# Gate maps of a PEER layer: one-hots of the first key on three engines, VectorE's instructions over eight tokens

## The reference

```
e1 = jnp.take_along_axis(i1, si // PEER_TOPK, axis=-1)
e2 = jnp.take_along_axis(i2, si % PEER_TOPK, axis=-1)
experts = e1 * N_KEYS + e2
gates = jax.nn.softmax(sv, axis=-1)
a = jnp.einsum('cd,ced->ce', h_c, u[e_c])
act = jax.nn.gelu(a, approximate=False) * g_c
return jnp.einsum('ce,ced->cd', act, v[e_c])
```

## Time and profile before

| | |
|---|---|
| runs of the kernel | 2482.23 us median of 3 (2481.68 to 2483.88) |
| the profiled execution | 2480.07 us, span 2478.3 us, mean granted clock of TensorE 0.982 |
| busy: PE, DVE, ACT, POOL | 93%, 70%, 52%, 9% of the span |
| chain that ended last | PE 81%, POOL 9%, DVE 5%, ACT 3% |
| line 432, GpSimd | 256 instructions, 212.5 us busy |
| lines 1425, 1429, 1437, VectorE | one-hots of i1, one-hots of i2, applies |
| line 1036, ScalarE | 512 instructions, 162.5 us busy, 390 ns each |

### The profile page before, as it was taken

One profiled execution on the slowest core, in us unless ns is written; L12 is line 12 of the kernel. 1 busy time (PEld: TensorE's weight loads), 2 busy tenths in 40 slices (PEclk: granted clock), 3 DMA queues, 4 the chain that ended last, 5 costly groups with the idle time before them and its releaser, 6 DMA issues.

```text
span 2478.3 us, 47911 instructions
## 1 busy us (share of the span) xinstructions
PE 2302.9 (93%) x15320; PEld 2099.6 (85%) x15320; DVE 1723.4 (70%) x3637; ACT 1284.0 (52%) x2842; POOL 226.9 (9%) x285
## 2 busy tenths in 40 slices
PE   5998999999996699999899999999999976999998
PEld 5896899999996588888788878999999965788887
DVE  7575666888868966666635557458888879666665
ACT  3454345455556755555546553445555567555554
POOL 0000000000007900000000000000000059100000
PEclk8998999999998999999999999999999989999999
DMA  9650354555550065555323324445555510455554
GB/s 371 260 196 35 107 199 148 183 178 184 184 183 25 0 203 194 191 191 193 128 102 136 120 103 142 145 143 182 185 180 184 179 67 0 144 195 192 191 192 152
DMA packets 106078, 389.71 MB, mean 157 GB/s; under 512 B 12032, under 2 KB 12160, under 8 KB 105232
## 3 DMA queue, kind: packets, MB, share of 16 engines
q1 hardware_dynamic: 104688, 381.73, 44.8%
q10 hardware_dynamic: 992, 4.88, 0.5%
q0 software_dynamic: 320, 2.13, 0.2%
HBM read 387.64 MB, written 1.05 MB: 157 GB/s over the span
## 4 chain that ended last, share of the span: by engine, by line
PE 81%; POOL 9%; DVE 5%; ACT 3%; DMA 1%; issue 1%; SPq 0%; POOLq 0%; DVEq 0%; ACTq 0%
PE ps L580 19%; PE ps L542 16%; PE ps L547 16%; PE ps L544 16%; PE ps L584 9%; POOL scores L432 9%; DMA big<-ada_in 1%; DVE act_lo L1272 1%; DVE lo L1195 1%; DVE big L1279 1%; PE ps L694 1%; PE ps L641 1%; PE ps L661 1%; DVE act_hi L1271 1%; ACT hi L923 0%
## 5 line engine op out<-in xcount | busy, mean ns | idle before, releaser
L923 ACT ACTIVATE hi<-raw 128x512 fp32r<-128x512 f32 x1356 | 776.5, 620 | 79.3 <-PE ps L547 77.0
L1195 DVE TENSOR_TENSOR lo<-raw,hi 128x512 fp32r<-128x512 f32 x844 | 547.0, 689 | 186.7 <-ACT hi L923 185.8
L542 PE MATMUL ps<-act_hi,hi 128*128 128x256 f32 x3376 | 553.3, 287 | 22.4 <-ACT hi L923 15.2
L547 PE MATMUL ps<-act_hi,lo 128*128 128x256 f32 x3376 | 546.6, 285 | 11.1 <-DVE lo L1195 11.1
L544 PE MATMUL ps<-act_lo,hi 128*128 128x256 f32 x3376 | 545.8, 284 | 0.0
L542 PEld LDWEIGHTS ps<-act_hi,hi 128*128 128x128 f32 x3376 | 468.5, 193 | 37.4 <-issue 20.2
L547 PEld LDWEIGHTS ps<-act_hi,lo 128*128 128x128 f32 x3376 | 469.0, 193 | 12.6 <-DVE lo L1195 12.6
L544 PEld LDWEIGHTS ps<-act_lo,hi 128*128 128x128 f32 x3376 | 468.8, 193 | 0.0
L1471 DVE TENSOR_TENSOR lo<-raw,hi 128x512 fp32r<-128x512 f32 x512 | 329.9, 688 | 131.4 <-ACT hi L923 124.2
L950 ACT ACTIVATE big<-ps 128x256 f32 (+1 forms) x346 | 133.1, 385 | 537.8 <-PE ps L547 537.8
L580 PE MATMUL ps<-hi,act_hi 128*128 128x512 f32 x1024 | 399.0, 390 | 0.0
(11 more groups left out here) (183 smaller groups left out, 1407.1 us busy)
## 6 DMA issues: line engine op xcount, KB each, us to landing
raw<-u SPq DMA_DIRECT2D x256, 512.0 KB, 4.2
raw<-v SPq DMA_DIRECT2D x256, 512.0 KB, 3.4
raw<-front SPq DMA_DIRECT2D x166, 512.0 KB, 3.5
big<-ada_in SPq DMA_DIRECT2D x48, 512.0 KB, 5.5
big<-biasA_in ACTq DMA_DIRECT2D x1, 2048.0 KB, 9.3
xT<-xT_in ACTq DMA_DIRECT2D x1, 1024.0 KB, 10.4
big<-keys_in ACTq DMA_DIRECT2D x1, 1024.0 KB, 12.7
scores<-memT_in POOLq DMA_DIRECT2D x1, 1024.0 KB, 5.4
```

The lines of the kernel that those rows point to most:

```text
L542: pe.matmul(out_ap, hi_l(k), hi_r(k), start=(first and k == 0), stop=False, skip_group_check=True)
L547: mm = pe.matmul(out_ap, lo_l(k), hi_r(k), start=False, stop=(last and k == n - 1), skip_group_check=True)
L923: act.activation(hi[:, s, :, :], raw[:, rs, 4 * h:4 * h + 4, :], ACT.Copy).then_inc(hi_done, 1)
L1195: dve.tensor_tensor(lo[:, s, :, :], raw[:, rs, 4 * h:4 * h + 4, :], hi[:, s, :, :].bitcast(F32), ALU.subtract).then_inc(lo_done, 1)
```

## The change

It does four things.

- The one-hots of i1 are shared by three engines, per group of 16 tokens: VectorE makes map 0 (4 tokens), GpSimd map 1 and two tokens of map 3 (`POOL_HOTS`), ScalarE map 2 and the other two tokens of map 3 (`ACT_HOTS`).
- GpSimd's and ScalarE's one-hots of i1 are scaled by the gate when they are made. GpSimd compares and multiplies in one instruction with two scalar columns. ScalarE takes two instructions per token: the distance |key - iota| (Abs), and Relu(gate - gate x distance), which is the gate where the distance is zero and zero elsewhere, as the gate is positive; it reads `neg_gate`, a new tile that VectorE makes before `ch_t`. Only map 0 still has its one-hots of i2 scaled by ScalarE, four instructions per group instead of 16.
- VectorE makes the one-hots of i2 of two maps (eight tokens) in one instruction of 1024 columns, and applies two maps, which lie in two neighbouring banks, in one instruction. `w_done` and `hot2` count pairs.
- The tile `zeros` of 256 columns becomes four columns, which its readers repeat.

```diff
@@ -46,6 +46,8 @@
 LN_EXP = "natural_log_exp_and_others"
 EXP_TANH = "exp_and_others"
 MAPS = 4
+POOL_HOTS = ((1, 4), (3, 2))
+ACT_HOTS = ((2, range(4)), (3, range(2, 4)))
 
 
 class Run:
@@ -176,7 +178,8 @@
         ones = sb("ones", [P, P])
         blockones = sb("blockones", [P, P])
         iota = sb("iota", [P, P])
-        zeros = sb("zeros", [P, T])
+        zero = sb("zero", [P, 4])
+        neg_gate = sb("neg_gate", [P, T])
         cols = sb("cols", [P, N_COLS])
         mod = sb("mod", [P, 48])
         gain = sb("gain", [P, 2, KT])
...
@@ -424,17 +428,17 @@
                 pool.wait_ge(ch_t, b)
 
                 for g in range(64 // MAPS):
-                    for j in range(1, MAPS, 2):
+                    for j, n in POOL_HOTS:
                         if g:
                             pool.wait_ge(wmap, 64 * (b - 1) + MAPS * (g - 1) + j + 1)
-                        for t in range(4):
+                        for t in range(n):
                             tok = 4 * MAPS * g + 4 * j + t
-                            ins = pool.tensor_scalar(onehot[:, j, t, :], iota[:, :], chosenT[:, 0, tok:tok + 1], None,
-                                                     ALU.is_equal)
-                        ins.then_inc(hot_odd, 1)
+                            ins = pool.tensor_scalar(onehot[:, j, t, :], iota[:, :], chosenT[:, 0, tok:tok + 1],
+                                                     chosenT[:, 2, tok:tok + 1], ALU.is_equal, ALU.mult)
+                        ins.then_inc(hot_pool, 1)
 
             link(pool.memset(ones[:, :], 1.0))
-            link(pool.memset(zeros[:, :], 0.0))
+            link(pool.memset(zero[:, :], 0.0))
             link(pool.memset(eps[:, :], EPS))
             link(pool.memset(ident[:, :], 0.0))
             link(select(ident[:, :], [[-1, P]], 0, 1, 1.0, ALU.not_equal))
...
@@ -706,10 +710,18 @@
                 def body(g):
                     for j in range(MAPS):
                         n = g * MAPS + (64 * (b - 1) + j)
-                        pe.wait_ge(hot_odd if j % 2 else hot_even, g * (MAPS // 2) + (32 * (b - 1) + j // 2 + 1))
-                        pe.wait_ge(hot_gate, n + 1)
-                        if not is_static(n) or n >= MAPS:
-                            pe.wait_ge(w_done, n - MAPS + 1)
+                        if j == 0:
+                            pe.wait_ge(hot_first, g + (16 * (b - 1) + 1))
+                            pe.wait_ge(hot_scaled, g + (16 * (b - 1) + 1))
+                        for k, (slot, _) in enumerate(POOL_HOTS):
+                            if slot == j:
+                                pe.wait_ge(hot_pool, g * len(POOL_HOTS) + (64 // MAPS * len(POOL_HOTS) * (b - 1) + k + 1))
+                        for k, (slot, _) in enumerate(ACT_HOTS):
+                            if slot == j:
+                                pe.wait_ge(hot_act, g * len(ACT_HOTS) + (64 // MAPS * len(ACT_HOTS) * (b - 1) + k + 1))
+                        pe.wait_ge(hot2, g * 2 + (32 * (b - 1) + j // 2 + 1))
+                        if not is_static(g) or g > 0 or b > 1:
+                            pe.wait_ge(w_done, g * 2 + (32 * (b - 1) + j // 2 - 1))
                         for t in range(4):
                             mm = pe.matmul(maps[j][:, t * P:t * P + P], onehot[:, j, t, :], gatehot[:, j, t, :],
                                            start=True, stop=True)
@@ -727,7 +739,7 @@
 
                 pe.wait_ge(ch_t, b)
                 for d in range(KT):
-                    pe.matmul(acc[:, d, :], zeros[:, 0:P], zeros[:, :], start=(d % 2 == 0), stop=False,
+                    pe.matmul(acc[:, d, :], zero[:, 0:1].broadcast_to([P, P]), zero[:, 0:1].broadcast_to([P, T]), start=(d % 2 == 0), stop=False,
                               skip_group_check=True)
                 run(f"v{b}")
                 for half in range(2):
@@ -1029,19 +1041,34 @@
                 act.wait_ge(ch_t, b)
 
                 def gate_hots(g):
-                    for j in range(MAPS):
-                        act.wait_ge(hot2, g * MAPS + (64 * (b - 1) + j + 1))
-                        for t in range(4):
+
+                    act.wait_ge(hot2, g * 2 + (32 * (b - 1) + 1))
+                    for t in range(4):
+                        ins = act.activation(gatehot[:, 0, t, :], gatehot[:, 0, t, :], ACT.Copy,
+                                             scale=chosenT[:, 2, bass.ds(g * 4 * MAPS + t, 1)])
+                    ins.then_inc(hot_scaled, 1)
+                    n = sum(len(tokens) for _, tokens in ACT_HOTS)
+                    done = 64 // MAPS * n * (b - 1)
+                    for j, tokens in ACT_HOTS:
+                        if not is_static(g):
+                            act.wait_ge(wmap, g * MAPS + (64 * (b - 1) - MAPS + j + 1))
+                        for t in tokens:
+                            act.activation(onehot[:, j, t, :], iota[:, :], ACT.Abs, scale=-1.0,
+                                           bias=chosenT[:, 0, bass.ds(g * 4 * MAPS + (4 * j + t), 1)])\
+                                .then_inc(hot_abs, 1)
+                        for t in tokens:
+                            done += 1
                             tok = g * 4 * MAPS + (4 * j + t)
-                            ins = act.activation(gatehot[:, j, t, :], gatehot[:, j, t, :], ACT.Copy,
-                                                 scale=chosenT[:, 2, bass.ds(tok, 1)])
-                        ins.then_inc(hot_gate, 1)
+                            act.wait_ge(hot_abs, g * n + done)
+                            ins = act.activation(onehot[:, j, t, :], onehot[:, j, t, :], ACT.Relu,
+                                                 scale=neg_gate[:, bass.ds(tok, 1)], bias=chosenT[:, 2, bass.ds(tok, 1)])
+                        ins.then_inc(hot_act, 1)
 
                 gate_hots(0)
                 with act.Fori(1, 64 // MAPS) as g:
                     gate_hots(g)
                 r = RUNS[f"v{b}"]
-                act.wait_ge(w_done, 64 * b)
+                act.wait_ge(w_done, 32 * b)
 
                 def body(g):
                     for j in range(GROUP):
...
@@ -1411,40 +1438,40 @@
                     .then_inc(gate_done, 1)
                 dve.wait_ge(ch_tr, b)
                 for c in range(3):
-                    ins = dve.tensor_copy(chosenT[:, c, :], bx[c][:, 0:T])
-                link(ins)
+                    dve.tensor_copy(chosenT[:, c, :], bx[c][:, 0:T])
+                link(dve.tensor_scalar(neg_gate[:, :], bx[2][:, 0:T], -1.0, None, ALU.mult))
                 dve.engine_nop().then_inc(ch_t, 1)
 
                 dve.wait_ge(taken, r.out0 + r.outs)
 
-                def hots(g, j):
-
-
-                    if j % 2 == 0:
-                        key = chosenT[:, 0, bass.ds(g * 4 * MAPS + 4 * j, 4)]
-                        dve.tensor_tensor(onehot[:, j, :, :], iota[:, :].unsqueeze(1).broadcast_to([P, 4, P]),
+                def hots(g, pair):
+
+                    key = chosenT[:, 1, bass.ds(g * 4 * MAPS + 8 * pair, 8)]
+                    dve.tensor_tensor(gatehot[:, 2 * pair:2 * pair + 2, :, :].rearrange("p b t n -> p (b t) n"),
+                                      iota[:, :].unsqueeze(1).broadcast_to([P, 8, P]),
+                                      key.unsqueeze(2).broadcast_to([P, 8, P]), ALU.is_equal).then_inc(hot2, 1)
+                    if pair == 0:
+                        key = chosenT[:, 0, bass.ds(g * 4 * MAPS, 4)]
+                        dve.tensor_tensor(onehot[:, 0, :, :], iota[:, :].unsqueeze(1).broadcast_to([P, 4, P]),
                                           key.unsqueeze(2).broadcast_to([P, 4, P]), ALU.is_equal)\
-                            .then_inc(hot_even, 1)
-                    key = chosenT[:, 1, bass.ds(g * 4 * MAPS + 4 * j, 4)]
-                    dve.tensor_tensor(gatehot[:, j, :, :], iota[:, :].unsqueeze(1).broadcast_to([P, 4, P]),
-                                      key.unsqueeze(2).broadcast_to([P, 4, P]), ALU.is_equal).then_inc(hot2, 1)
-
-                def apply(g, j):
-
-                    n = g * MAPS + (64 * (b - 1) + j)
-                    dve.wait_ge(wmap, n + 1)
-                    d = dense[:, :, bass.ds(g * 4 * MAPS + 4 * j, 4)]
-                    dve.tensor_tensor(d, maps[j].rearrange("p (t i) -> p i t", t=4), d, ALU.mult)\
-                        .then_inc(w_done, 1)
-
-                for j in range(MAPS):
-                    hots(0, j)
+                            .then_inc(hot_first, 1)
+
+                def apply(g, pair):
+
+                    dve.wait_ge(wmap, g * MAPS + (64 * (b - 1) + 2 * pair + 2))
+                    d = dense[:, :, bass.ds(g * 4 * MAPS + 8 * pair, 8)]
+                    first = (6, 0)[pair]
+                    dve.tensor_tensor(d, ps[:, first:first + 2, :].rearrange("p b (t i) -> p i (b t)", t=4), d,
+                                      ALU.mult).then_inc(w_done, 1)
+
+                for pair in range(2):
+                    hots(0, pair)
```

(10 more changed lines are left out.)

9 lines of the change are left out of this document (5 added, 4 removed).

## The result

The changed kernel takes 2496.32 us, median of four runs (2494.98 to 2498.41); the kernel before took 2481.95 in four runs beside it (2480.71 to 2483.88). The ratio is 1.0059, with a 95% interval of 1.0043 to 1.0075. So the change costs 14.4 us where 7 us of gain were forecast. The time lies above the range, on the other side of no change, and on the 2496 that the GpSimd rival had with the upper end of its price. The profiled execution took 2494.98 us, span 2493.1, mean granted clock 0.976 (before 0.982).

What follows compares the result with a forecast made beforehand. GpSimd was taken as the bound, to be replaced by a circle of waits: per block 0.35 + 6.3 + 15 x 6.2 + 1.5 + 2.75 = 103.9 us against 107.6, two blocks -7.4, giving 2475 us, range 2468 to 2489.

Steps and rivals of the forecast that it cites:

- the GpSimd rival: GpSimd's six one-hots per group become the bound again, from a load of 6.45 us: 2487 or 2496 us, chance 0.18.
- GpSimd's load: GpSimd's six one-hots per group, with second column and waits behind VectorE: 5.8 us, ends 5.1 and 7.7.
- the circle: Loop of waits through VectorE, ScalarE and TensorE, apply to next apply of maps 0 and 1: 6.19, taken as 6.2 us.
- the sign of "wrong": Prediction wrong if a GpSimd instruction alone exceeds 0.79 us, VectorE's 1024 columns 1.3, or even-part clock is below 0.95.
- The sign of the GpSimd rival: In the new profile, GpSimd without gaps and above 1.05 us per instruction would show GpSimd as the bound.
- The second column: GpSimd's one-hots: extra for a second scalar column and multiply, taken as 0.1 us each, ends 0 and 0.29.
- The waits: GpSimd held up by VectorE instructions with two SBUF inputs, in proportion to columns: 1.7 us per group.
- The prediction's other price: GpSimd's hold-up if a 1024-column VectorE instruction always costs its full length: 1.07 us each, 2.5 per group.
- VectorE and ScalarE: Their loads per group: VectorE 5.1 us, ScalarE 5.3 us, with 0.30 per distance or scaling and 0.38 per Relu.
- The first apply: Start of each block's stretch: first apply begins 6.3 us in, set by TensorE at its lower clock level.
- The end of the stretch: From the last apply of maps 0 and 1, through maps 2 and 3, to the zero matmuls: 2.75 us.
- The clock: TensorE's granted clock: 1.00 in the even part, one fall after the first group, counted as 1.5 us per block.

Runs made afterwards that it cites:

- The PSUM version of the kernel before: Kernel before the change, with only `iota`, the row of key numbers VectorE compares with, copied to a PSUM bank: 2460.91 us, ratio 0.9919.
- the version with one column: Changed kernel, but GpSimd's six one-hots per group only compare, with one scalar column and no multiply: 2475.35 us, ratio 0.9975.
- the versions at 6.32: Changed kernel with GpSimd's one-hots only comparing (2475.35 us), with `iota` in PSUM (2475.51), or with one token moved from GpSimd to ScalarE (2479.86).
- the split over four tokens: Changed kernel with VectorE's instructions back over four tokens: 2490.40 us; with `iota` in PSUM as well: 2441.28 us.
- either part of the change alone: Changed kernel with VectorE's instructions back over four tokens: 2490.40 us; kernel before with only VectorE's i2 one-hots and applies paired: 2507.06 us.

## Why the prediction was wrong, point by point

**What bounds the kernel now: right.** GpSimd did, and VectorE stood close behind it. The PSUM version of the kernel before shows the distance: 6.56 to 5.98.

**GpSimd's load, "6 x (0.58 + 0.1) + 1.7 = 5.8 us": this is the step that failed.** It measured 6 x 0.785 + 2.1 = 6.8, so GpSimd stayed the bound and the circle did not take over. Two terms were undersized, and by the sum both are needed. With 0.19 for the second column and 1.7 of waits the load would be 6 x 0.77 + 1.7 = 6.3, just at the circle; with 0.1 and 2.1 it would be 6.2. The load passed 6.45, the point from which the GpSimd rival decided, and went on to the 6.9 for which that rival had 2496. The prediction had set the sign of "wrong" at more than 0.79 us for an instruction alone; it measured 0.78 to 0.79 (0.797 at most with `iota` in PSUM), just at that sign. The sign of the GpSimd rival came plainly: 1.14 us per instruction, above its 1.05, and hardly a gap.

*The second column.* Taken 0.1, measured 0.19 (780 against 593 ns, with nothing else changed). I had put it near zero because one short read is small beside a tensor read. The multiply over 128 elements was counted at nothing, and there was no reason for that. The upper end of 0.29, the difference of a whole instruction to a select, is itself a slip (597 - 288 is 0.31; 0.29 is 0.58 - 0.288). The 0.19 lies halfway between it and the 0.1 taken. With the middle of both ranges, 0.145 for the column and 2.05 for the waits, the load would have been 6.4, above the circle.

The Trainium skill, GPSIMD Engine Reference, section 7 (Performance pitfalls for Q7 kernels), gives about 102 cycles for a small read command, from which the prediction had worked out the estimate of 0.085 us. The runs show 0.19 for column and multiply together; how it divides was not measured. A rule on the price of a read is no price of an instruction with one read more and one operation more.

*The waits.* Taken 1.7 per group, measured 2.1. The prediction had said that an apply does not hold GpSimd up and one-hots with both inputs in SBUF do. That is shown: with `iota` in PSUM no instruction of GpSimd exceeds 0.82 us. The size came from columns, 0.32 us per 512. That does not hold: the same 2560 columns cost 2.1 us in two instructions of 1024 and one of 512 and also in five of 512, 2.3 in the former cut beside the shorter instruction of GpSimd, and 1.3 (5 x (1.048 - 0.785)) where GpSimd has five tokens. What a wait costs goes by where it starts: in the version with one column 30 instructions start 0.03 to 0.04 us before a 1024 that a 512 follows and each takes 1.64, that is 1.04 more than the 0.60 alone; with five tokens 30 start 0.36 us into one and take 2.04, 1.25 more than 0.785. The prediction's other price, 1.07 for a 1024, is close to the first, though no row of it gives that figure.

The Trainium skill, SBUF — State Buffer, "Who interferes with whom", calls the shared port an exclusive lock. The trace agrees: one instruction of GpSimd stands through two of VectorE (2.26 us) and one, at the start of each block, through three (3.34 us). By the lock in full I had 2.5 us and a load of 6.6; measured 2.1 and 6.8. The rule was nearer than my proportion, and it should have had more than its part of 0.18.

**The circle, 6.19 us: nearly right.** It is 6.32. Apply to one-hots 1.15, one-hots 1.21, two maps 2.05, scalings 1.28, TensorE to VectorE 0.14 were as computed. ScalarE started 0.16 us after the one-hots ended instead of 0.13, and TensorE 0.33 after the scalings (807.57 against 805.96 + 1.28) instead of 0.24: the handover had been read behind GpSimd and was used behind ScalarE. At 6.32 in each round and the load in time, the time is the forecast's: 2475.35 and 2475.51 were measured.

**VectorE and ScalarE: right.** 1024 columns take 1.22 us as read from the earlier trace rows. The Relu takes 479 ns beside 387 for a distance, 0.09 more, where 0.08 was taken. ScalarE's load never set the pace: it stood idle for 15.8 of 60 us until VectorE's one-hots came.

**The first apply: wrong.** It came 8.07 us after `chosenT` was ready, not 6.3. I had let TensorE's lower clock set it, with the maps of ScalarE's scalings at 2.75. What came last was GpSimd's fourth one-hot (760.43 + 5.68), because its first waits behind all of VectorE's opening: 1024, 512 and 1024 columns without a gap between them. Only then follow eight passes, 2.09 us at the lower level. Without that wait the figure was right: 6.40 and 6.21 us in the two blocks with `iota` in PSUM.

**The end of the stretch: 0.75 us better than taken.** From the last apply of maps 0 and 1 to the zero matmuls it is 1.75 and 2.28 us instead of 2.75. The zero matmuls with a repeated column take 3.48 us (3.46 before): free, as costed.

**The clock.** One fall was taken, behind the first group; it did not come (the clock was 1.00 from 769.8 to 786.8, across an idle stretch of TensorE of 1.75 us up to 772.52), and four others did in each block. They came with GpSimd's late rounds, not with the circle: the versions at 6.32 have none in the even part. The price of 1.4 us for a round is contained in the mean of 6.90.

Together, per block: 15 x (6.90 - 6.2) = 10.5, less the 1.5 counted apart for the clock, first apply +1.8, end -0.75: 10 us, for two blocks 20. From the 2472.7 of the sum that gives 2493, and with the 2.4 us ahead of the first stretch the 2495 of the profiled execution.

**The chances.** The case that came had 0.18, the forecast 0.42. Its load lay 0.4 below the circle by two terms that no row showed, each with an upper end beyond it; that is too little distance for 0.42 against 0.18. The range ended at a load of 6.7, while the text itself priced 6.9.

## What to carry to other kernels

Before work is moved off an engine, write its load with the upper ends of all unknown terms at once; if that sum crosses the next bound, the sign is open. Cutting the count of instructions on the bounding engine by a quarter is no gain if each of those left becomes a third dearer (0.59 to 0.78 us here). Where VectorE and GpSimd work side by side, one input of VectorE's instruction in PSUM frees GpSimd: it was worth 21 us in the kernel before and 49 us in the split over four tokens, where either part of the change alone cost time. And pairing instructions over two banks saves a little issue time, but ties the work of the pair to one wait, which closed a circle of 6.32 us where VectorE's own load was 5.1.
